# Weight remainders of the layer attentions: subtracted on GpSimd in place of VectorE

## The reference

```python
hx = modulate(rms_norm_2(x, norm_mix[l]), sh_m, sc_m)
px = jnp.split(hx @ w_in[l], SPLIT_IDX, axis=-1)
...
p = jax.nn.softmax(s, axis=-1)
w = (p[:, :, 0] - lam * p[:, :, 1]).astype(v.dtype)      # differential attention
return jnp.einsum("bhqk,bhkd->bhqd", w, v)
...
p = jax.nn.softmax(s, axis=-1).astype(v.dtype)           # grouped-query attention
return jnp.einsum("bhgqk,bhkd->bhgqd", p, v)
...
gates = jax.nn.sigmoid(zgate.reshape(b, l, N_BRANCH, D_MODEL))
ys = jnp.stack([y_four, y_conv, y_gqa, y_diff], axis=2)
return jnp.sum(gates * ys, axis=2) @ lp["w_out"]
```

## Time and profile before

| what | value |
|---|---|
| runs | 2266.43, 2271.29, 2271.88 us (median 2271.29) |
| the profiled execution, from the first to the last instruction | 2257.7 us |
| median less that span | 13.6 us |
| busy: TensorE, VectorE, ScalarE, GpSimd | 2116.4, 1607.2, 1012.0, 301.3 us |
| share in the chain that ended last: TensorE, VectorE, ScalarE, GpSimd | 74, 16, 4, 1% |
| weight remainders on VectorE (line 452) | 293 of 2302 ns mean, 674.0 us busy |
| granted TensorE clock, mean | 0.980 of full speed |

### The profile page before, as it was taken

How to read it: one execution, slowest core, us unless ns; L and a number is a source line. 1 busy time by engine, 2 the same in 40 slices (tenths; PEclk the granted TensorE clock), 3 DMA queues, 4 the chain that set the end, 5 groups by cost and what they waited for, 6 DMA issues and landing times.

```text
span 2257.7 us, 41393 instructions
## 1 busy us (share of the span) xinstructions
PE 2116.4 (94%) x16941; PEld 1983.8 (88%) x16941; DVE 1607.2 (71%) x2112; ACT 1012.0 (45%) x1207; POOL 301.3 (13%) x291
## 2 busy tenths in 40 slices
PE   7899999899889999999999879999999987999998
PEld 6666897799779999999999778999999986799998
DVE  8987657688776755655679877675557996866554
ACT  4112546544644533434444465454344445544432
POOL 3772004100110100100101210020020021000000
PEclk9999999999989999999999989999999998999999
DMA  8679766656334565555666323456556642344652
GB/s 258 237 272 326 248 237 214 216 170 187 99 113 150 179 197 187 184 186 195 196 188 189 117 94 94 151 181 195 186 177 184 181 138 75 94 131 150 195 195 75
DMA packets 292260, 397.40 MB, mean 176 GB/s; under 512 B 9270, under 2 KB 257293, under 8 KB 285453
## 3 DMA queue, kind: packets, MB, share of 16 engines
q1 hardware_dynamic: 285620, 383.53, 52.1%
q0 software_dynamic: 3008, 5.56, 1.1%
q10 hardware_dynamic: 3480, 6.18, 0.8%
HBM read 387.53 MB, written 3.15 MB: 173 GB/s over the span
## 4 chain that ended last, share of the span: by engine, by line
PE 74%; DVE 16%; ACT 4%; issue 3%; DMA 2%; POOL 1%; DVEq 0%; SPq 0%; ACTq 0%; POOLq 0%
PE L L937 61%; DVE w_rest L452 4%; PE M L937 3%; PE L L1198 2%; PE L L1184 2%; PE M L1447 1%; DVE work L2790 1%; PE L L1211 1%; DVE m L2107 1%; DMA raw<-in_w_ada 1%; PE L L1267 1%; DVE work_r L2246 1%; ACT w_high L446 1%; DVE work L2689 1%; DVE soft L2220 1%
## 5 line engine op out<-in xcount | busy, mean ns | idle before, releaser
L937 PE MATMUL L<-n_high,w_high 128*128 128x256 f32 x3104 | 877.1, 283 | 11.7 <-DVE n_rest L2116 4.9
L937 PE MATMUL L<-n_rest,w_high 128*128 128x256 f32 x3104 | 865.0, 279 | 0.0
L937 PE MATMUL L<-n_high,w_rest 128*128 128x256 f32 x3104 | 864.9, 279 | 0.0
L452 DVE TENSOR_TENSOR w_rest<-raw,w_high 128x2048 fp32r<-128x2048 f32 x293 | 674.0, 2302 | 203.6 <-PE L L937 193.6
L446 ACT ACTIVATE w_high<-raw 128x2048 fp32r<-128x2048 f32 x293 | 561.2, 1916 | 333.8 <-PE L L937 298.5
L937 PEld LDWEIGHTS L<-n_high,w_high 128*128 128x128 f32 x3104 | 588.7, 190 | 29.7 <-issue 21.4
L937 PEld LDWEIGHTS L<-n_high,w_rest 128*128 128x128 f32 x3104 | 588.5, 190 | 0.0
L937 PEld LDWEIGHTS L<-n_rest,w_high 128*128 128x128 f32 x3104 | 588.0, 189 | 0.4
L937 PE MATMUL L<-hid_high,w_high 128*128 128x256 f32 x768 | 215.3, 280 | 4.2 <-DVEq L2588 4.2
L937 PE MATMUL L<-hid_high,w_rest 128*128 128x256 f32 x768 | 214.1, 279 | 0.0
L937 PE MATMUL L<-hid_rest,w_high 128*128 128x256 f32 x704 | 196.3, 279 | 0.0
(11 more groups left out here) (412 smaller groups left out, 2986.3 us busy)
## 6 DMA issues: line engine op xcount, KB each, us to landing
raw<-in_w_in SPq DMA_DIRECT2D x116, 1024.0 KB, 5.5
raw<-in_w_ffn SPq DMA_DIRECT2D x99, 1024.0 KB, 5.2
raw<-in_w_ada SPq DMA_DIRECT2D x32, 1024.0 KB, 6.5
raw<-in_w_out SPq DMA_DIRECT2D x16, 1024.0 KB, 5.2
raw<-in_w_gate SPq DMA_DIRECT2D x11, 1024.0 KB, 5.3
raw<-in_w_up SPq DMA_DIRECT2D x11, 1024.0 KB, 5.3
raw<-in_w_down SPq DMA_DIRECT2D x11, 1024.0 KB, 4.9
work<-in_w_ada SPq DMA_DIRECT2D x8, 1024.0 KB, 7.4
```

Of the source, the lines that this page charges most:

```text
L452: nc.vector.tensor_tensor(w_rest[:, u.first % 2, :], raw[:, u.first % 4, :], w_high[:, u.first % 4, :].bitcast(F32), ALU.subtract).then_in ...
L937: ins = mm(dst, a, b, start=first and i == 0, stop=last and i == 2, skip_group_check=skip)
```

## The change

GpSimd makes the remainders of 15 units in each of the three passes: those that VectorE made inside its two attention loops (6 at `diff`, 9 at `gqa`), 45 in all, of 128x2048 each. The operation, its operands and the semaphores stay the same. GpSimd comes to them in `next_weights(key, at)`, behind the operand remainders of the same task, and in addition waits until `rest_ready` shows that all remainders before it are made. VectorE's `unit_ended` in the loops only merges. Behind the attentions VectorE takes the remainders up again, and waits once for GpSimd's last.

```diff
--- before.py
+++ after.py
@@ -446,10 +446,13 @@
             nc.scalar.activation(w_high[:, u.first % 4, :], raw[:, u.first % 4, :], ACT.Copy).then_inc(high_ready, 1)
 
         def split_rest(dve, u):
-            dve.wait_ge(high_ready, u.count(1))
+            split_rest_on(dve, nc.vector, u)
+
+        def split_rest_on(queue, engine, u):
+            queue.wait_ge(high_ready, u.count(1))
             if u.first >= 2:
-                dve.wait_ge(unit_done, u.count(-1))
-            nc.vector.tensor_tensor(w_rest[:, u.first % 2, :], raw[:, u.first % 4, :],
+                queue.wait_ge(unit_done, u.count(-1))
+            engine.tensor_tensor(w_rest[:, u.first % 2, :], raw[:, u.first % 4, :],
                                     w_high[:, u.first % 4, :].bitcast(F32), ALU.subtract).then_inc(rest_ready, 1)
 
         def ahead_high(act, u, last):
@@ -893,6 +896,23 @@
                     for a in range(2):
                         pool.dma_start(kdup[HEAD * a:HEAD * (a + 1), h, at:at + T], qk[HEAD * h:HEAD * (h + 1), HC, :]).then_inc(kd_in, 16)
 
+            def weight_rest(u):
+
+                pool.wait_ge(rest_ready, u.count())
+                split_rest_on(pool, nc.gpsimd, u)
+
+            def next_weights(key, at):
+
+                if kind_of(key) == "diff":
+                    if at == 0:
+                        weight_rest(Unit(FIRST[fill_units(key)[0][0]] + 1))
+                    ended = () if at % 2 else (at - 2, at - 1)
+                else:
+                    ended = (at - 1,)
+                for end in ended:
+                    for name, k in ended_at(key, end) if end >= -1 else ():
+                        weight_rest(Unit(FIRST[name] + k + 2))
+
             for key in TASKS:
                 if key[2:] == "diff":
                     if key[:2] in ROPE_OF:
@@ -904,6 +924,10 @@
                         high, rest = split_of(key, what, h)
                         pool.wait_ge(op_high, done)
                         nc.gpsimd.tensor_tensor(rest, src, high.bitcast(F32), ALU.subtract).then_inc(op_rest, 1)
+                    next_weights(key, at)
+                for end in (len(TASKS[key]), len(TASKS[key]) + 1) if kind_of(key) == "diff" else (len(TASKS[key]),):
+                    if kind_of(key) != "diff" or end % 2 == 0:
+                        next_weights(key, end)
                 for k in NORMS_BEHIND.get(key, ()):
                     add_squares(k)
                 if key == "mem":
@@ -2179,7 +2203,10 @@
                 if name[2:6] == "proj":
                     merge_unit(name, k)
                 if more:
-                    ahead_rest(dve, Unit(FIRST[name] + k + 1), UNITS)
+                    next_ = Unit(FIRST[name] + k + 1)
+                    if (name[2:], k) == ("gate2", 2):
+                        dve.wait_ge(rest_ready, next_.count(1))
+                    ahead_rest(dve, next_, UNITS)
 
             def add_to_h(name, h, gain, beside={}, until={}):
 
@@ -2267,11 +2294,9 @@
                             turned_rest(x)
                     elif i + 2 < len(tasks):
                         negative_max(tasks[i + 2])
-                    if i == 0 and kind_of(key) == "diff":
-                        ahead_rest(dve, Unit(FIRST[fill_units(key)[0][0]]), UNITS)
                     for at in (i - 1,) if kind_of(key) != "diff" else () if i % 2 else (i - 2, i - 1):
                         for name, k in ended_at(key, at) if at >= -1 else ():
-                            unit_ended(name, k)
+                            unit_ended(name, k, more=False)
                     if i in beside:
                         beside[i]()
                 if kind_of(key) != "diff":
```

## The result

The changed kernel takes 2329.3 us (median of 4 runs, 2318.1 to 2332.9), beside 2268.9 us for the kernel before on the same chip (4 runs, 2266.0 to 2271.9). The ratio is 1.026, with a 95% interval of 1.024 to 1.029: 60 us slower. The forecast was 2311 us, 42 us above the same runs of before; the range ended at 2326 and is missed by 3 us.

The account below looks back on a forecast made before the run. TensorE was taken to bound the kernel outside the attentions, VectorE's softmax chain the differential ones, nearly TensorE the grouped. 12.4 us in c0 and 13.8 each in x0 and x1 made 40, on 2271.3: 2311 us; range 2268 to 2326.

Parts of the forecast that it names:

- Place 5: Start of each grouped attention: the 128x1 product for ScalarE's maximum waits, +3.1 us in each of three passes.
- its rule: A GpSimd operation reading on-chip memory holds VectorE operations with two on-chip operands to its end, up to 4.6 us.
- rival C: At the 13 places, GpSimd gives way within a long operation, so holds are short: 2241 to 2256 us; chance 0.10.
- The remaining units of the grouped attention: Units covered by 9 to 10 us of matmuls, next weights already scaled: 0, give or take 1 us each.
- 7.4 + 2 x 5.9: Grouped attentions: 3.1 us at the start of each, then head norms, 4.3 in c0 and 2.8 in x0 and x1.
- Place 3: Unit 3 in the differential attention: VectorE has passed the pair operation and goes on with PSUM, nothing waits: 0.
- their terms: Differential attentions, at gate1 units 1 and 2 and proj1 unit 0: c0 0.7, 3.3, 1.0; x0 and x1 3.5, 3.4, 1.0.
- The clock: Attention stretches at 0.94 to 0.95: every hundredth lost would be 5 us more, left for the range.
- the 13 subtractions: Moved subtractions on the chain, 3 in c0, 5 each in x0 and x1: removal gives at most 29.8 us.
- The 13.6 us outside the first and last instruction: Median of timed runs above the profiled span, taken as time outside the instructions; changes were added to the median.
- rival A: Grouped attentions' 128x1 products are not held, taking 14.9 us off: 25 us slower, 2296 us; chance 0.20.
- 4.3 us in the grouped attention of c0: Head norms in c0: GpSimd meets the scaling for which the transposes wait, +4.3 us.

Follow-up runs that it names:

- e5: Changed kernel with each GpSimd subtraction cut into four 128x512 operations back to back, no waits between; 2285.0 us, ratio 1.009 to the kernel before.
- e4: Changed kernel with the grouped attentions' 128x1 product made as a scaling by a per-partition scalar; 2291.2 us, ratio 1.012 to the kernel before.
- e11: Changed kernel with only the grouped attentions' subtractions on GpSimd, uncut, and the 128x1 product using a per-partition scalar; 2260.8 us, ratio 0.9991 to the kernel before.
- e3: Changed kernel with two GpSimd memsets of 128x2048 replacing each subtraction, so GpSimd only writes; 2257.1 us, ratio 0.996 to the kernel before.

## Why the prediction was too low

**The mechanism and its price were right.** GpSimd's subtraction takes 4.63 us at the mean (4.585 at the median), the sum had 4.6. At each of the places that the sum named in c0 and x0, the named operation is held, for a time within 0.4 us of the one worked out; in x1 the taps are 0.8 us off. (The figure of the Trainium skill, "GPSIMD Engine Reference", "Performance versus the Vector engine", that the prediction gave, 4497 ns, was 0.1 us below the measured median.) Two of its steps were less firm than they read. Place 5 by its own rows is 1343.5 - 1340.57 = 2.9 us and not 3.1, and 2.9 was measured in x0. And its rule was drawn for operations with two operands, while the sum held scalings too, which have one, without a row for it. The trace of before has such a row, beside a GpSimd operation that began at 1288.99:

```profile
1289.22 1.33 DVE L2237 TENSOR_SCALAR work<-work,soft 128x512 f32<-128x512 f32 x1
```

That scaling takes 0.49 us undisturbed. The sign was right, and rival C is answered: VectorE gets in at the end of an operation and not within it (e5), and one operation of 4.6 us is longer than the 2.3 us that it replaces.

**The step that failed: "The remaining units of the grouped attention ... 0, give or take 1 us each".** It looked at the scaling alone, which is indeed mostly done when the unit ends. It didn't ask for the other operation with two on-chip operands that each task has, the 128x1 product. 14 products beyond those of the sum were held, by some 32 us in all. And it took 9 to 10 us of matmuls per unit as cover, although the merge that frees TensorE's bank stands behind the product in VectorE's queue: the chain shows the stand at 1443.19. The grouped attentions were priced at 7.4 + 2 x 5.9 = 19.2 us and grew by 35; with the product in the other form they grow by nothing (e4, e11), so that the products and what is queued behind them are shown to be all of it. The 4.89 us scaling at 1467.24 fell under the same sentence, but holds of that kind cost nothing that can be told: e11 has them (up to 4.4 us long) and is no slower than before.

**Place 3.** It was read in x0, where it does cost nothing, and written for all passes. In c0 the maxima and exponentials are half as long, and GpSimd's 4.57 us from 596.71 meet the pair operation (4.69 us instead of 0.48). But it explains little: the differential attentions (+29) exceed their terms (5.0 + 2 x 7.9 = 20.8) by 8 us, and of these c0, which grew by 7, has only 2. The other 6 lie in x0 (+12) and x1 (+10), and no run tells what they are.

**The clock,** which the sum left to the range. TensorE is busy 18 us longer for the same matmuls in these stretches, at clocks of 0.83 to 0.92 instead of 0.89 to 0.96. Not all of this is on the path, and it isn't independent: with the product's holds gone, the grouped stretches have TensorE at 239.3 us, below the 242.9 of before. It is what a hold costs beyond its length once TensorE stands, as at 1446.18, where it was 0.6 us on 2.1. How much of the 60 us this is can't be told apart from the holds.

**Perhaps too much credit for what was removed.** Taking the 13 subtractions off the chain was credited at 2.3 us at most places. e3 has them all off and no two-operand hold, and is 0.4% faster, some 9 us, with its scalings still held. How much more the holds of the scalings hide, no run tells.

**The base.** The 13.6 us outside the first and last instruction were no such thing: after the change the profiled run took 1.8 us more than its span (2332.9 and 2331.1), and the run of before with a span of 2257.7 us took 2259.5. So the execution profiled before was merely shorter than the median. The sum used the median, so this moved nothing.

Nothing was found for rival A (products not held); where e4 makes it true, 26 us more than before are measured, near its 25. In part that is luck: its 25 had 4.3 us in the grouped attention of c0, which in e4 is no longer than before (77 us), as the scaling meant there isn't held (0.52 us at 669.01); the differential attentions make up for it, with 26 us more by the profile instead of 20.8.

## What to carry to other kernels

Before work goes to GpSimd, list every VectorE operation that reads two tiles of on-chip memory, however small, and ask for each one what is queued behind it on VectorE; a free engine is no proof of a free move. Cut the moved operation into short pieces, since a hold lasts to the end of one operation (but a row of short operations can meet every piece), and turn small products into the form with a scalar of each partition. Look for operations that are 0.16 us long and stand ahead of a bank release, as these are worth 30 us here and don't appear in any list of costly ones.

## What the runs showed of the hardware

- A multiplication of 128x1 by a scalar of each partition isn't held by a reading GpSimd operation (longest of 48: 219 ns in e4, where 22 of them began while GpSimd was at work), the same multiplication with two operands is (3708 ns). A 128x512 scaling of the same kind with a scalar is held, by 4.4 us at 1467.24. No run here tells whether its size or something else in its form decides.
- GpSimd's subtraction takes 0.74, 1.29 and 4.6 us at 256, 512 and 2048 elements of each partition: about 2.2 us for each 1024 and some 0.2 us for an operation. So eight pieces cost 5.9 us instead of 4.6.
- A held operation need not have started later. At 1467.24 the scaling starts 0.02 us ahead of GpSimd's subtraction (1467.26) and waits for it all the same.
- The row of the operation on eight columns that waited through six of GpSimd's stays open: in e5 nothing waited through more than one of four that stand back to back.
- VectorE's merging sum (L2197, two on-chip operands) is held in e4 too, by up to 2.3 us. The waits for this line are the same before, after and in e4 (15.2 us, 9 times), so no one waits longer for it.
- VectorE's maxima and turned remainders read PSUM and aren't held. In the changed kernel 27 turned remainders began while GpSimd was at work and took 0.42 to 0.69 us, as those beside them without it.
